# Three attention stages: repeated products on TensorE ahead of the first units, and two value projections moved behind the compressed scores

## The reference, cut to what matters

```python
s_c = einsum('bgrqd,bgnd->bgrqn', qc, kc) - slopes * dist_c      # compressed: 15 blocks
p_c = masked_softmax(s_c, dist_c >= 0)
o_c = einsum('bgrqn,bgnd->bgrqd', p_c, vc)
...                                                              # selected: ks, vs
...                                                              # window: kw, vw
o = gc[..., 0:1] * o_c + gc[..., 1:2] * o_s + gc[..., 2:3] * o_w
```

## Time and profile before

| | us |
|---|---|
| median of three runs | 4190.16 (4181.4 to 4198.37) |
| the profiled execution, own time | 4185.95 |
| its span in the trace | 4184.1 |
| PE busy (matmul) | 3883.7 |
| DVE busy | 2695.6 |
| ACT busy | 1814.7 |
| mean granted TensorE clock | 0.922 |

### The profile page before, as it was taken

How to read it: one execution, slowest core, us unless ns; L and a number is a source line. 1 busy time by engine, 2 the same in 40 slices (tenths; PEclk the granted TensorE clock), 3 DMA queues, 4 the chain that set the end, 5 groups by cost and what they waited for, 6 DMA issues and landing times.

```text
span 4184.1 us, 69331 instructions
## 1 busy us (share of the span) xinstructions
PE 3883.7 (93%) x28928; PEld 3543.7 (85%) x28928; DVE 2695.6 (64%) x4831; ACT 1814.7 (43%) x3088; POOL 1456.6 (35%) x848
## 2 busy tenths in 40 slices
PE   7999997999989889989999989989999999999899
PEld 6658997689979867779999959989869998867699
DVE  4437886578877775567777867777658644675543
ACT  3233444444454442244545635444445444332343
POOL 2004443044434440034444423444314444320243
PEclk9759998699989989989999999999969999979899
DMA  5105662157647420036665315657516644210143
GB/s 207 56 1 201 257 267 96 58 213 267 249 168 270 171 92 1 1 135 262 231 268 192 142 46 219 260 212 265 187 61 249 250 180 148 96 41 1 46 169 114
DMA packets 63688, 664.38 MB, mean 159 GB/s; under 512 B 7056, under 2 KB 7568, under 8 KB 7952
## 3 DMA queue, kind: packets, MB, share of 16 engines
q1 hardware_dynamic: 63376, 659.94, 42.0%
HBM read 658.86 MB, written 1.05 MB: 158 GB/s over the span
## 4 chain that ended last, share of the span: by engine, by line
PE 72%; DVE 19%; ACT 5%; issue 2%; POOL 1%; DMA 0%; SPq 0%; DVEq 0%; ACTq 0%; POOLq 0%
PE pb L275 70%; DVE wp L228 5%; DVE ada_acc L240 3%; PE pb L282 3%; ACT wp L266 3%; DVE wk L240 2%; DVE wk L228 2%; DVE sq L228 1%; DVE sq L240 1%; DVE hT L240 1%; ACT wk L266 1%; ACT sq L266 1%; DVE hx L240 1%; DVE rsb L228 0%; POOL sq L228 0%
## 5 line engine op out<-in xcount | busy, mean ns | idle before, releaser
L275 PE MATMUL pb<-hx,wp 128*128 128x256 f32 x15744 | 1992.6, 287 | 96.1 <-DVE hx L240 40.5
L275 PEld LDWEIGHTS pb<-hx,wp 128*128 128x128 f32 x15744 | 1955.2, 195 | 116.7 <-issue 104.0
L228 POOL TENSOR_TENSOR wp<-ring,wp 128x512 fp32r<-128x512 f32 (+1 forms) x596 | 1242.6, 2102 | 1984.1 <-ACT wp L266 1942.6
L228 DVE TENSOR_TENSOR wp<-ring,wp 128x1024 fp32r<-128x1024 f32 (+1 forms) x670 | 824.8, 1252 | 359.8 <-ACT wp L266 359.0
L266 ACT ACTIVATE wp<-ring 128x1024 fp32r<-128x1024 f32 x936 | 938.2, 1046 | 235.0 <-PE pb L275 227.7
L275 PE MATMUL pb<-ex,wp 128*128 128x256 f32 x5856 | 758.3, 287 | 23.7 <-DVE ex L228 23.7
L275 PEld LDWEIGHTS pb<-ex,wp 128*128 128x128 f32 x5856 | 730.0, 194 | 25.3 <-issue 19.8
L240 DVE SCALAR_TENSOR_TENSOR ada_acc<-ring,cact,ada_acc 128x384 f32<-128x384 f32 x576 | 528.9, 982 | 39.6 <-ACT ada_acc L266 39.6
L275 PE MATMUL pb<-wk 128*128 128x128 f32 (+8 forms) x3136 | 491.7, 328 | 15.6 <-ACT wk L266 6.6
L275 PEld LDWEIGHTS pb<-wk 128*128 128x128 f32 (+4 forms) x3136 | 342.6, 192 | 160.1 <-issue 96.9
L228 DVE TENSOR_TENSOR sq<-sq,pb 128x256 f32<-128x256 f32 (+1 forms) x360 | 161.2, 449 | 323.0 <-ACT sq L266 272.9
(11 more groups left out here) (177 smaller groups left out, 2810.6 us busy)
## 6 DMA issues: line engine op xcount, KB each, us to landing
ring<-weights SPq DMA_DIRECT2D x385, 1536.0 KB, 6.7
ring<-weights SPq DMA_DIRECT2D x41, 1024.0 KB, 4.9
ring<-weights SPq DMA_DIRECT2D x4, 512.0 KB, 10.3
cst<-consts SPq DMA_DIRECT2D x1, 2032.0 KB, 11.8
ring<-weights SPq DMA_DIRECT2D x1, 1280.0 KB, 5.9
prm<-params SPq DMA_DIRECT2D x1, 1258.0 KB, 7.4
ring<-weights SPq DMA_DIRECT2D x1, 1152.0 KB, 4.9
xT<-xT_in SPq DMA_DIRECT2D x1, 1024.0 KB, 4.8
```

Of the source, the lines that this page charges most:

```text
L228: return self.real.tensor_tensor(out, a, b, op) if self.real else Uncounted()
L275: return self.real.matmul(out, l, r, start=start, stop=stop, skip_group_check=skip)
```

## The change

A helper `repeated_pe` writes `n` fp32 products of two constants (`ones` 128x128 as weights, the identity 128x128 as moving operand) into a PSUM bank that the program has just taken and will overwrite. In every attention stage it is called ahead of the scores of units 0, 5 and 6 (8, 3 and 2 products), ahead of the values of unit 0 (4) and ahead of the transposes of unit 0 (10): 27 products in each of three stages. Each call stands ahead of the `wait_ge` on data that follows it.

In NSA the projection vS leaves its place ahead of the spreads; vS now stands between scores and transposes of the first half, and vW between those of the second. ACT does the exponential of each half first and copies vS or vW out behind it, and it loads the table set that has the exponential right behind the gate's sigmoid.

```diff
     def attention_pe(e, st, units, off):
+    def repeated_pe(e, ps, n):
+        for _ in range(n):
+            e.mm(ps[:, 0:128], ones[:, 0:128], ident, True, True, skip=True)
+    BEFORE_SCORES, BEFORE_TURN, BEFORE_VALUES = {0: 8, 5: 3, 6: 2}, 10, 4
...
                 ps = bk.take(e, (st, "s", i), (v_out, (st, "s", i)))
+                repeated_pe(e, ps, BEFORE_SCORES.get(i, 0))
                 e.wait_ge(*v_out[u.q_key])
...
                 start = u.first
+                if n == 0:
+                    repeated_pe(e, pb[m % 2], BEFORE_VALUES)
                 for sig, event in u.ready:
...
                 b = att_scores(off, n)
+                if n == 0:
+                    repeated_pe(e, ps, BEFORE_TURN)
                 e.wait_ge(*v_step[st, "unit", n])
...
             tokens_pe(e, "gate", c_gate, 48)
-            tokens_pe(e, "vS", c_v[0], 256)
             for k in range(8):
...
                     ins.then_inc(*scored.up((st, "cs", qb, hp)))
-                if qb == 0:
-                    tokens_pe(e, "vW", c_v[1], 256)
+                tokens_pe(e, ("vS", "vW")[qb], c_v[qb], 256)
                 for h4 in range(4):
...
             tokens_act(e, "gate", gts, 48, ACT.Sigmoid)
-            tokens_act(e, "vS", vS, 256, ACT.Copy)
+            e.tables("natural_log_exp_and_others")
             for qb in range(2):
-                if qb == 0:
-                    tokens_act(e, "vW", vW, 256, ACT.Copy)
                 e.wait_ge(*v_step[st, "cdiff", qb])
                 e.act(cs, cs, ACT.Exp).then_inc(*a_step.up((st, "cexp", qb)))
+                tokens_act(e, ("vS", "vW")[qb], (vS, vW)[qb], 256, ACT.Copy)
```

## The result

The changed kernel takes 4083.89 us (median of 4 runs, 4081.8 to 4088.53) against 4187.85 before (4 runs): ratio 0.9754, 95% interval 0.9743 to 0.9766, about 104 us less. The forecast was 4086. The profiled execution has a span of 4086.7 us where it was 4184.1, 97.4 less, at a mean clock of 0.951 instead of 0.922.

What follows compares the result with a forecast made beforehand. TensorE's half clock was taken to bound the attention units. NSA -56.4, MoBA -21.8 and third -22.1 us sum to -100, from 4185.95 to 4086; range 4063 to 4150.

Steps and rivals of the forecast that it cites:

- What bounds the stages: In the three attention stages TensorE's half clock sets the pace, not its work and not DVE.
- my 0.57: Ratio of a unit's time at full clock to half, from one group of records; bounds exact halving and 0.65.
- The units with their products: First transposes to last values: NSA 76.6, MoBA and third 33.4 each, plus 1 us a stage for nine uncovered products.
- To the first transposes: Delay of unit 0's transposes by the added products: +2.4 us in NSA, +3.6 in MoBA, +3.2 in the third.
- The clock comes up and holds: Full clock reached and held over the units of all three attention stages; chance 0.70.
- a guess from two rises: MoBA's clock rises around its scores, judged from rises near 123.4 (vS) and 167.8 (transposes) in NSA.
- The first rival: Clock falls behind the repeated products or never rises: 4210, or 4199 if it rises first; chance within a shared 0.10.
- The moved projections: Moving vS and vW in NSA: -2 us, bounds 0 and -6, +5 if vS runs at half to its end.
- the second half: NSA's second half partly at full clock: up to 3.1 us off scores, 2 off vW, 0.9 off transposes.
- The loss on the spreads: Without vS ahead, NSA's spreads run at half clock: 4.69 us becomes 9.4.
- The output projection: Behind the units it begins at full clock: -1.3 us in MoBA, -1.1 in the third, nothing in NSA.

Runs made afterwards that it cites:

- The run without the nine: The full change less the nine products behind unit 0's first transposes (ahead of values 0 and scores 5 and 6), leaving 18 a stage: 4074.72 us, ratio 0.9729.
- The narrow products: The full change with each repeated product reading 16 partitions instead of 128, same number and columns: 4207.4 us, ratio 1.0047 against the kernel before.
- the blocks in mid-stage: Ahead of unit 8's scores: 20 broad products instead of those at the start, 4103.3 us (0.9797); or 24 16-partition products added to the full change, 4193.28 (1.0015).

## Why the prediction was right, point by point

- **What bounds the stages**: right. At full clock a steady pair of NSA's units takes 4.82 us (two steps, 185.38 to 190.20) and MoBA's unit 2.12, where it was 8.8 and 3.88: a ratio of 0.55, nearer to halving than my 0.57. Over the whole stretches, without the nine products, the ratios are 0.56, 0.58 and 0.59 (75.13, 34.13 and 34.50 us of 134.4, 58.51 and 58.60): waits at the two ends stay as they were, such as the 0.58 us ahead of the last values, which stands there at both clocks. DVE did not become the bound.
- **The units with their products**: forecast 77.6, 34.4 and 34.4 us from the first transposes to the last values, measured 77.34, 35.47 and 35.51. The run without the nine parts the two terms. The units alone take 75.13, 34.13 and 34.50 where I had 76.6, 33.4 and 33.4: the one ratio was too high for NSA and too low for the others. The nine products cost 2.2, 1.3 and 1.0 where I took 1 each: half of them was covered in MoBA and the third, where unit 0's values would have waited 0.74 and 1.14 us for ACT's copy, and next to nothing in NSA.
- **To the first transposes**: +2.5 in NSA, +2.9 in MoBA (8.46 us from 696.32 to 704.78, against 5.51 before) and +2.8 in the third, forecast +2.4, +3.6 and +3.2. The price of a product was right: 0.23 at full and 0.46 at half.
- **The clock comes up and holds**: right in all three stages. The narrow products show that it takes more than a busy TensorE, the blocks in mid-stage that the units keep either level. That it would come up within MoBA's scores was a guess from two rises, and it came out so. The first rival, a fall behind the products, did not come in the change; the narrow kernel lands where it was priced, 4207 against 4210.
- **The moved projections**: the direction was right, the size was not. Forecast -2, bounds 0 to -6; measured 5.7 in the profile (6.33 between the starts of the units, less the 0.65 that gate began earlier) and 6.8 to 7.0 by the runs. The term that I undersized is the second half: both its scores (3.32) and its transposes (1.91) ran wholly at full clock, 4.3 us less than at half, where I gave about 2 to all of it. Part of this is the luck of one profile: in the kernel with the products alone, in the old order, these scores took 3.41 us as well. From the start of the gate projection to the units the two profiles in the old order have 51.42 and 48.16 us, those in the new one 44.02 to 45.75, so the move is worth between 2.4 and 7.4 by the profiles. The loss on the spreads, 4.1 us, was forecast as 4.7.
- **The output projection**: 24.31 us to 23.30 in the third, -1.0 where -1.1 was forecast; in MoBA 24.55 to 23.96, -0.6 for the forecast -1.3, as PE now waits 0.31 us for a split piece that was covered before.

The total is nearer than its terms: the three stages alone gave some 102 us in the profile, and about 5 came back outside them, 3.6 of it between MoBA's output projection and the spreads of the third attention, where the change touches nothing. Why is open; the four executions of each kernel spread by 17 and 7 us, so that the profile's difference (97.4) and that of the medians (104) are both within what a single execution can be off. It was also not tried whether a full clock over the recurrences, which show the remaining low slices, could be had in the same way.

## What to carry to other kernels

Read the granted clock beside the busy time: a stage in which TensorE is busy without a gap may be running at half, and if its own work keeps either level, a few microseconds of dense products at the right place can take two fifths off the time of its units, as here. Put them where the pipeline fills, in waits that stand anyway, and then take away as many as the profile allows: here 17 of 27 could go, and they cost time; with only four left the third attention lost the clock again. A real product that is moved can do the same work for nothing, and can lose it where it stood before.

## What the runs showed of the hardware

- The clock follows products by the partitions that they read: with 27 products from 128 partitions it was at 1.00 over the units of all three stages, with 27 from 16, of the same length, at 0.50 (ratio 0.9754 against 1.0047). Transposes of 128 partitions counted like products (0.9745).
- A stage has two stable speeds: NSA's units at 4.40 and at 2.41 us each with the same instructions, changed into one another by 5.82 us of dense and 6.38 us of thin products.
- Scores of neighbouring units from different halves of the partitions overlap. In MoBA the units alternate between the halves, in NSA two in a row share one. With the same 16 records at full clock, the first four units' scores took 1.69 us in MoBA (693.04) and 2.34 in NSA (162.46, both in the kernel with 18 products); in line they would take 2.8, an estimate from 0.23 us for 128 columns.
